# The end of a hybrid decoder layer, redone by tokens: TensorE turns x1 and then y, one operation per part scales and adds, and one store changes its place in SyncE's order

## The reference, cut to what matters

```python
def rmsnorm(x, g):
    y = xf * lax.rsqrt(jnp.mean(xf * xf, axis=-1, keepdims=True) + EPS)
    return (y * g.astype(jnp.float32)).astype(x.dtype)

def ffn_sublayer(x, w_up, w_down, g_pre, g_post):
    h = rmsnorm(x, g_pre)
    a = jnp.square(jax.nn.relu(jnp.einsum('ntd,df->ntf', h, w_up)))
    return x + rmsnorm(jnp.einsum('ntf,fd->ntd', a, w_down), g_post)
```

## Time and profile before

| what | us |
|---|---|
| median of 3 runs | 2083.25 |
| lowest, highest | 2081.37, 2084.26 |
| profiled execution, its own time | 2083.59 |
| its span | 2081.9 |
| PE busy / DVE / ACT / POOL | 1975.1 / 1329.2 / 1223.2 / 945.8 |
| mean granted TensorE clock (share of full speed) | 0.964 |

### The profile page before, as it was taken

How to read it: one execution, slowest core, us unless ns; L and a number is a source line. 1 busy time by engine, 2 the same in 40 slices (tenths; PEclk the granted TensorE clock), 3 DMA queues, 4 the chain that set the end, 5 groups by cost and what they waited for, 6 DMA issues and landing times.

```text
span 2081.9 us, 39222 instructions
## 1 busy us (share of the span) xinstructions
PE 1975.1 (95%) x15342; PEld 1944.4 (93%) x15342; DVE 1329.2 (64%) x1958; ACT 1223.2 (59%) x1790; POOL 945.8 (45%) x646
## 2 busy tenths in 40 slices
PE   7999999899964999999999999989999999999995
PEld 7999999899944999999999999989999999999994
DVE  3455643522258777777777777666666666666676
ACT  5234421422224677777777777667777777777782
POOL 0000022211161767676767677544445555444574
PEclk9999998999966999999999999989999999999996
DMA  5421121242220565656566665875655555556532
GB/s 174 158 62 61 52 82 56 102 146 92 92 86 17 170 208 175 209 182 196 186 192 191 192 199 183 292 250 188 205 181 200 191 184 204 183 183 205 187 105 86
DMA packets 270767, 328.16 MB, mean 158 GB/s; under 512 B 8128, under 2 KB 236872, under 8 KB 268975
## 3 DMA queue, kind: packets, MB, share of 16 engines
q1 hardware_dynamic: 267104, 315.66, 46.6%
q10 hardware_dynamic: 3479, 9.99, 1.3%
HBM read 253.79 MB, written 74.22 MB: 158 GB/s over the span
## 4 chain that ended last, share of the span: by engine, by line
PE 91%; DVE 5%; POOL 1%; DMA 1%; issue 1%; ACT 0%; SPq 0%; DVEq 0%; POOLq 0%; ACTq 0%
PE banks L1968 21%; PE banks L1613 21%; PE banks L1970 21%; PE banks L1969 21%; PE banks L1758 1%; POOL sq_sum L699 1%; DVE xF L1556 1%; PE banks L1579 1%; PE banks L1728 1%; DMA mlp_kept<-mlp_sums 1%; PE banks L1746 1%; DVE x1T L1481 1%; DVE h_part L1497 1%; DVE h_sum L1492 0%; PE banks L1587 0%
## 5 line engine op out<-in xcount | busy, mean ns | idle before, releaser
L1968 PE MATMUL banks<-h_part,splits 128*128 128x272 f32 x1792 | 522.9, 292 | 28.4 <-DVE h_part L1497 17.1
L1968 PE MATMUL banks<-mlp_parts,splits 128*128 128x272 f32 x1792 | 518.4, 289 | 12.2 <-DVE y_sum L1450 11.4
L1970 PE MATMUL banks<-h_part,splits 128*128 128x272 f32 x1792 | 521.3, 291 | 0.0
L1969 PE MATMUL banks<-h_part,splits 128*128 128x272 f32 x1792 | 518.8, 289 | 0.0
L1970 PE MATMUL banks<-mlp_parts,splits 128*128 128x272 f32 x1792 | 518.1, 289 | 0.0
L1969 PE MATMUL banks<-mlp_parts,splits 128*128 128x272 f32 x1792 | 517.2, 289 | 0.0
L1968 PEld LDWEIGHTS banks<-h_part,splits 128*128 128x128 f32 x1792 | 340.3, 190 | 29.4 <-issue 20.2
L1968 PEld LDWEIGHTS banks<-mlp_parts,splits 128*128 128x128 f32 x1792 | 337.9, 189 | 12.5 <-issue 11.6
L1969 PEld LDWEIGHTS banks<-mlp_parts,splits 128*128 128x128 f32 x1792 | 342.1, 191 | 0.0
L1969 PEld LDWEIGHTS banks<-h_part,splits 128*128 128x128 f32 x1792 | 340.8, 190 | 0.0
L1970 PEld LDWEIGHTS banks<-h_part,splits 128*128 128x128 f32 x1792 | 340.0, 190 | 0.0
(11 more groups left out here) (234 smaller groups left out, 3469.7 us busy)
## 6 DMA issues: line engine op xcount, KB each, us to landing
raw_up<-in_w_up SPq DMA_DIRECT2D x128, 512.0 KB, 7.7
raw_down<-in_w_down SPq DMA_DIRECT2D x128, 512.0 KB, 4.4
mlp_parts<-mlp_kept SPq DMA_DIRECT2D x56, 1088.0 KB, 8.4
mlp_kept<-mlp_hi SPq DMA_DIRECT2D x32, 952.0 KB, 4.5
mlp_kept<-mlp_sums SPq DMA_DIRECT2D x32, 952.0 KB, 5.7
w_raw<-in_w_in SPq DMA_DIRECT2D x40, 512.0 KB, 3.6
w_raw<-in_w_out SPq DMA_DIRECT2D x32, 512.0 KB, 3.4
x_kept<-x1T SPq DMA_DIRECT2D x4, 1088.0 KB, 4.0
```

The source lines that it names most:

```text
L1968: nc.tensor.matmul(out, wh, xh, start=first, stop=False, skip_group_check=not STARTS[i])
L1969: nc.tensor.matmul(out, wh, xl, start=False, stop=False, skip_group_check=not STARTS[i])
L1970: ins = nc.tensor.matmul(out, wl, xh, start=False, stop=j == pairs - 1, skip_group_check=not STARTS[i])
```

## The change

1. `store_lo` of group 30 moves: it was behind all load parts of the first chunk, now it stands ahead of part 4.
2. In the last chunk DVE multiplies finished y tiles by g_last in place (`scale_y`, 14 operations in the loop, two behind the last product of each group's index 5, and 2 after the last product).
3. After the last product PE turns x1 (80 transposes) into token rows, with the sums over partitions put behind part 6, then turns y (80 more). Banks 0 to 6 are a ring, bank 7 holds the sums.
4. ACT copies 14 of the x1 parts to x1_tok, DVE 6. The scale per token stays a column per token block (rstd); it is not spread by PE any more.
5. Of the y parts DVE takes 13 with one operation each (bank * rstd + x1_tok); for the other 7 ACT copies with the scale and POOL adds. The 20 stores read x1_tok and wait for no buffer.

```diff
@@ load parts of the first chunk, SyncE
                 if i == 2:
                     store_hi(UP_GROUPS - 2)
+                if i == 4:
+                    store_lo(UP_GROUPS - 2)
                 sp.wait_ge(product_done, N_UP - NP + i // 2 + 1)
                 load_part(0, i)
-            store_lo(UP_GROUPS - 2)
@@ who reads which part
-        OWN_NORMED = (0, 3, 7, 11, 14)
+        Y_RING = 7
+        Y_PARTS = TOK * KT // 4
+        X1_DVE = (1, 3, 5, 11, 14, 17)
+        Y_POOL = tuple(range(0, Y_PARTS, 3))
+        X1_ACT = tuple(o for o in range(Y_PARTS) if o not in X1_DVE)
+        Y_DVE = tuple(o for o in range(Y_PARTS) if o not in Y_POOL)
@@ stores, SyncE
+            for o in range(Y_PARTS):
+                kg, c = divmod(o, TOK)
+                who, count = y_reader(o)
+                sp.wait_ge(y_added[who], count)
...
+                sp.dma_start(dst[:, kg * 512:(kg + 1) * 512], x1_part(o)).then_inc(y_stored, 16)
@@ GpSimd
-            gp.wait_ge(scale_ready, 4)
-            for kt in range(KT):
-                if kt not in OWN_NORMED:
-                    normalise_tile(y_sum[:, kt, :], norm_f)
+            for i, o in enumerate(Y_POOL):
+                who, count = x1_reader(o)
+                gp.wait_ge(x1_copied[who], count)
+                gp.wait_ge(y_scaled, i + 1)
+                nc.gpsimd.tensor_tensor(x1_part(o), x1_part(o), y_tmp[0:tok_rows[o % TOK], i, :], ALU.add).then_inc(y_added[0], 1)
@@ ScalarE
+            for i, o in enumerate(X1_ACT):
+                act.wait_ge(y_turned, o + 1)
+                nc.scalar.activation(x1_part(o), y_bank(o, o), ACT.Copy).then_inc(x1_copied[0], 1)
+                if i == 5:
+                    take_root(3)
+            act.wait_ge(rstd_ready, 4)
+            for i, o in enumerate(Y_POOL):
+                act.wait_ge(y_turned, Y_PARTS + o + 1)
+                c = o % TOK
+                nc.scalar.activation(y_tmp[0:tok_rows[c], i, :], y_bank(Y_PARTS + o, o), ACT.Copy,
+                                     scale=rstd[0:tok_rows[c], c:c + 1]).then_inc(y_scaled, 1)
@@ VectorE
+            def scale_y(m):
+                dve.wait_ge(sq_ready, 2 * KT + m + 1)
+                nc.vector.tensor_scalar(y_sum[:, m, :], y_sum[:, m, :], g_last[:, m:m + 1], None, ALU.mult).then_inc(y_ready, 1)
...
+                G, i = divmod(N, NP)
+                n = G - (ALL_G - OUT_PAIRS)
+                if i == 5 and n > 0:
+                    scale_y(2 * n - 2)
+                    scale_y(2 * n - 1)
...
+            copy_x1(X1_DVE[0])
+            scale_y(KT - 2)
+            scale_y(KT - 1)
+            copy_x1(X1_DVE[1])
+            copy_x1(X1_DVE[2])
+            sums_by_token(3, banks[:, Y_RING, :])
+            row_roots(3)
+            dve.wait_ge(rstd_ready, 4)
+            for o in X1_DVE[3:]:
+                copy_x1(o)
+            for o in Y_DVE:
+                dve.wait_ge(y_turned, Y_PARTS + o + 1)
...
+                nc.vector.scalar_tensor_tensor(out=x1_part(o), in0=y_bank(Y_PARTS + o, o), scalar=rstd[0:tok_rows[c], c:c + 1],
+                                               in1=x1_part(o), op0=ALU.mult, op1=ALU.add).then_inc(y_added[1], 1)
@@ TensorE
-            turn_sums(3, total=sqf_sum, tmp=sqf_tmp)
-            spread_scales(3)
+            for o in range(Y_PARTS):
+                if o >= Y_RING:
+                    who, count = x1_reader(o - Y_RING)
+                    pe.wait_ge(x1_copied[who], count)
+                if o == Y_RING:
+                    turn_sums(3, banks[:, Y_RING, :], sqf_sum, sqf_tmp)
+                turn_part(o, xF)
+            pe.wait_ge(y_ready, KT)
+            for o in range(Y_PARTS):
...
+                turn_part(Y_PARTS + o, y_sum)
```

More of the change, by code:

```diff
@@ L215, in hybrid_decoder @@
         sqf_sum = at("sqf_sum", F_AT + 2 * T * 4, [P, T])
[L216 to L218 removed]
+        y_tmp = at("y_tmp", F_AT + 3 * T * 4, [P, 7, 512])
+        x1_tok = at("x1_tok", H_AT + NP * DOWN_J * 2 * H * 4, [P, TOK, D])
+        assert F_AT + 3 * T * 4 + 7 * 2048 <= H_AT + NP * DOWN_J * 2 * H * 4
         banks = ctx.enter_context(nc.psum_tensor("banks", [P, 8, 512], F32))
@@ L341, in hybrid_decoder @@
         y_turned = sem("y_turned")
-        y_copied = [sem("y_copied_act"), sem("y_copied_dve")]
-        y_stored = [sem(f"y_stored{i}") for i in range(8)]
+        x1_copied = [sem("x1_copied_act"), sem("x1_copied_dve")]
+        y_scaled = sem("y_scaled")
+        y_added = [sem("y_added_pool"), sem("y_added_dve")]
+        y_stored = sem("y_stored")
         kept = sem("kept")
@@ L369, in hybrid_decoder, with x1_reader, y_reader, y_bank @@
         START_SPLITS = {0: 0, 5: 1, 7: 2, 11: 3}
-        OWN_NORMED = (0, 3, 7, 11, 14)
[L375 to L379, removed]
+        Y_RING = 7
[4 more added lines that the diff above has]
+        Y_DVE = tuple(o for o in range(Y_PARTS) if o not in Y_POOL)
+        def x1_reader(o):
+            return (1, X1_DVE.index(o) + 1) if o in X1_DVE else (0, X1_ACT.index(o) + 1)
+        def y_reader(o):
+            return (0, Y_POOL.index(o) + 1) if o in Y_POOL else (1, Y_DVE.index(o) + 1)
+        def y_bank(s, o):
+            return banks[0:tok_rows[o % TOK], s % Y_RING, :]
+        def x1_part(o):
+            kg, c = divmod(o, TOK)
+            return x1_tok[0:tok_rows[c], c, kg * 512:(kg + 1) * 512]
         pool_order = [3, 2, 1, 0]
@@ L588, in _ @@
                     sp.dma_start(xF[:, 4 * n:4 * n + 4, :], x1_kept[:, 4 * n:4 * n + 4, :]).then_inc(x1_moved[n], 16)
[L591 to L601, removed]
+            for o in range(Y_PARTS):
+                kg, c = divmod(o, TOK)
+                who, count = y_reader(o)
+                sp.wait_ge(y_added[who], count)
+                dst = (y_prompt[0, c * P:(c + 1) * P, :] if c < TOK - 1 else y_sample.rearrange("b t d -> (b t) d"))
+                sp.dma_start(dst[:, kg * 512:(kg + 1) * 512], x1_part(o)).then_inc(y_stored, 16)
+            sp.wait_ge(y_stored, 16 * Y_PARTS)
             sp.wait_ge(kept, 16 * 3)
@@ L1542, in _ @@
                     mlp_low(UP_GROUPS - 1)
[L1545 to L1569, removed]
@@ L1978, in _, with turn_part @@
             pe.wait_ge(taken, N_ALL)
-            turn_sums(3, total=sqf_sum, tmp=sqf_tmp)
-            spread_scales(3)
-            pe.wait_ge(scale_ready, 4)
-            for kg in range(KT // 4):
-                for a in range(4):
-                    pe.wait_ge(y_ready, 4 * kg + a + 1)
-                    for c in range(TOK):
-                        o = kg * TOK + c
-                        r = tok_rows[c]
-                        if o >= 8 and a == 0:
-                            who, count = copier(o - 8)
-                            pe.wait_ge(y_copied[who], count)
-                        ins = nc.tensor.transpose(banks[0:r, o % 8, a * P:(a + 1) * P], xF[:, 4 * kg + a, c * P:c * P + r], ident[:])
-                        if a == 3:
-                            ins.then_inc(y_turned, 1)
+            for one in x1_moved:
+                pe.wait_ge(one, 32)
+            def turn_part(s, source):
+                kg, c = divmod(s % Y_PARTS, TOK)
+                r = tok_rows[c]
+                for a in range(4):
+                    ins = nc.tensor.transpose(y_bank(s, s % Y_PARTS)[:, a * P:(a + 1) * P],
+                                              source[:, 4 * kg + a, c * P:c * P + r], ident[:])
+                ins.then_inc(y_turned, 1)
+            for o in range(Y_PARTS):
[7 more added lines that the diff above has]
+            for o in range(Y_PARTS):
+                if o < Y_RING:
+                    who, count = x1_reader(Y_PARTS + o - Y_RING)
+                    pe.wait_ge(x1_copied[who], count)
+                else:
+                    who, count = y_reader(o - Y_RING)
+                    pe.wait_ge((y_scaled, y_added[1])[who], count)
+                turn_part(Y_PARTS + o, y_sum)
 _INS = ['x_prompt', 'x_sample', 'cache_k', 'cache_v', 'state_pool', 'w_in', 'w_out', 'w_pool', 'pool_scale', 'attn_sinks',
```

17 lines of the change are left out of this document (6 added, 11 removed).

## The result

The changed kernel takes 2060.72 us (median of 4 runs, 2059.18 to 2061.8), the kernel before in the same measurement 2083.48. The ratio is 0.9892, 95% interval 0.9875 to 0.9909: 22.8 us, 1.1%, faster. 2061.5 was forecast. The profiled execution took 2061.8 with a span of 2060.1 (before 2081.9) at a mean granted clock of 0.974 (before 0.964).

The account below looks back on a forecast made before the run. TensorE was taken as the bound through both weight stages, with no engine full in the end. Terms -8.8, +2.0 and -14.9 sum to -21.7; forecast 2061.5 us at 60%, own range 2055.5 to 2066, 8-in-10 range 2055.5 to 2070.5.

Parts of the forecast that it names:

- The moved store: Change from up to down: store lands at 1349.6 instead of 1358.4, DVE's squaring and all behind it earlier; -8.8 us.
- nothing was to be counted for the loads behind: Down stage start: three loads behind the store land some 2.5 us later, at most 0.7 us late; counted as nothing.
- The multiplications: Last chunk: a POOL operation between two DVE multiplications makes TensorE wait 0.35 us, six times; +2.0 us.
- the 2.65 us operation: Earlier profile: 272-column DVE operation, all operands in SBUF, begun while POOL worked; said to end with POOL's operation.
- The end: Behind the last product: new chain to the span's end, set by the stores, 29.7 us instead of 45.6; -14.9 us.
- the 1.0 set aside for the clock: Behind the last product: allowance of 1.0 us in case the clock falls behind the sums' one-column matmuls.
- The 0.65 us for a combination: Behind the last product: each of DVE's 13 combinations for y parts takes 0.65 us.
- Half clock to the end: Behind the last product: TensorE stays at half clock, the end gains only 2.4 us; 2074.1 us, 13%.
- The store landing before DVE asks: Change from up to down: queue shorter than counted, store gains 12.0 us; 2058.3 us, 13%.
- the store gaining nothing: Change from up to down: store not served before the loads behind it; 2070.3 us, 6%.
- DVE's combinations meeting POOL's additions: Behind the last product: 13 combinations at 1.77 us each, the end at 38.1 us; 2069.0 us, 6%.
- DVE falling behind in the last chunk: Last chunk: each multiplication waits out a POOL operation, TensorE loses 3.4 us per group and clock; 2091.6 us, 2%.

Follow-up runs that it names:

- the experiment: Changed kernel with each pair of the last chunk's multiplications made one group later, the last pair left in place; 2059.6 us, ratio 0.9889 to the kernel before.

## Why the forecast held

The time was right to 0.8 us, in part by luck: errors of up to 1.4 us, of both signs, cancelled, one of them (+1.05 in front of the change) being chance.

**The moved store, -8.8 against -7.7.** The mechanism was right: issue with the end of mlp_low, landing in the queue's turn, squaring at once, TensorE 2.0 later (1.97). What was mis-sized is the landing, 9.5 us behind the issue instead of 8.5. The store itself landed 2.7 us behind part 3, nearly the 2.5 that were counted; the rest is that part 3's landing was taken over unchanged from the earlier trace rows. It came 11.6 us behind its issue instead of 10.8, which looks as if the store's packets had begun beside part 3's; no run shows that. And the rate was lower with a store among the loads:

```profile
1342.20:1345.00 2.80, 2.80 (x25) 2.80 (x24) 2.38 (x5) 2.05 (x5) 1.14 (x1) 1.00 1.05 396
1345.00:1348.00 3.00, 3.00 (x26) 3.00 (x26) 1.31 (x3) 1.31 (x3) 1.30 (x1) 1.00 0.97 328
1348.00:1351.70 3.70, 2.15 (x18) 1.93 (x16) 0.00 (x0) 1.75 (x3) 0.00 (x0) 1.00 1.08 386
```

328 GB/s for three microseconds, where 399 had been counted: half a microsecond. That nothing was to be counted for the loads behind held: TensorE's second wait (1.68) is one on DVE, as forecast, and with the store put back behind all loads it is 1.69, so the three loads behind the store have no part in it.

**The multiplications, +2.0 against +0.6.** The mechanism was right again, POOL's operation between the two halves of a pair, and one of them only. The term was mis-sized in two places: the pair took 1.96 where 2.30 had been laid out, since POOL's operation began 0.2 after DVE's first and not behind it (of the 2.65 us operation the prediction says that it ended with POOL's; by the earlier trace rows it ended 0.3 behind it, as the multiplication here); and a take and a low part in a row move DVE on by 0.95 (2010.26 to 2011.21) and not by the 1.12 of their durations, as one is begun before the other is written down as ended. Together 0.5 us, more than the 0.35 of wait that each of six groups was to pay. That a multiplication is 0.43 us was nearly right (0.49 to 0.51 alone).

**The end, -14.9 against -15.7.** The chain came out as laid down: 0.58 before the first transpose, 3.1 for the first seven parts, 2.0 for the sums, 5.7 for the other x1 parts, the first store issued 14.2 behind the last take (13.9 forecast), the stores gapless at 322 to 347 GB/s, 1.8 behind the last data. Only the 1.0 set aside for the clock was not needed: with 28 transposes in front, sums of 2.0 us left it at 1.00. The 0.65 us for a combination, for which the prediction names no row, held (13 in 8.64 us). No run takes the new end further apart: what the missing spreading of the scale and the combinations from PSUM are worth each for itself is worked out from rows and not tested. The lower end of the stated range adds up to 2055.2 and not 2055.5, which changes nothing.

**The rivals.** Half clock to the end: no, 1.00 throughout. The store landing before DVE asks, and the store gaining nothing: no, DVE waited 4.22 us where near 3 was forecast. DVE's combinations meeting POOL's additions: no, 732 ns each with POOL at work beside them,

```profile
L794 POOL TENSOR_TENSOR x_tok<-x_tok,y_tmp 128x512 f32<-128x512 f32 (+1 forms) x7 | 8.9, 1273 | 10.5 <-ACT y_tmp L1087 10.3
L1585 DVE SCALAR_TENSOR_TENSOR x_tok<-banks,rstd,x_tok 128x512 f32<-128x512 f32 (+1 forms) x13 | 8.6, 732 | 1.1 <-PE banks L2002 1.1
```

where four combinations had taken 7.08 in the kernel before. That the operand in PSUM makes the difference fits this and the earlier trace rows; no run changes the operand alone. DVE falling behind in the last chunk: no. What came nearest to it is the 2.03 us pair of the experiment, and that cost 0.7 in one group.

## What to carry to other kernels

A store that frees a buffer somebody is about to write belongs in the queue behind only as many loads as the reader needs before that moment; count the queue's content at its issue, and look at what the loads behind it will then hold up. Where an end is bound by stores, its length is the time to the first store plus the transfer, so make the first output early rather than all of it fast; and put work that needs no one in front of a matmul that must wait, since an idle TensorE can cost the clock as well as the wait. What a fallen clock costs depends on what comes next: some 1.6 us where nothing waited behind it (686.5 against 684.9 in the two traces of the store ahead of part 3), nothing where TensorE had to wait for DVE soon after. When a DVE operation with all operands in SBUF has to stand beside POOL, place it in POOL's gap, and check the last round, where POOL does something else.

## What the runs showed of the hardware that was not expected

- After TensorE had been idle for 2.8 us the clock stayed at 1.00 for another microsecond of work and only then fell to 0.50, for some 7 us. In the wait of 3.65 us at the change from up to down it fell while TensorE was still idle (0.95 on average from 1352.0 to 1353.8, 0.50 from there to 1357). A wait of 1.89 us left it at 1.00 in one execution (matmuls of 0.36 and 0.29 us behind it), while in another it fell with a wait of 1.94 us (0.57), after waits of 0.50 and 1.12.
- With one store of 952 KB among the loads the queue's rate fell some 2 us behind the store's issue, in each kernel that had it there: 328 GB/s over 3 us in the changed kernel, 297 over 2 us with the store alone moved, 290 to 297 over 4 us with the store one load further ahead, against 391 in that stretch of the kernel before. Why was not tried.
- A kernel's part in front of an edit isn't the same in two executions: the same code reached the moved store's issue anywhere from 1338.5 to 1344.3 us. Stretches of a trace leave that part out, but one trace isn't enough either: for the same edit, the store ahead of part 3, they gave 3.1 us in one measurement and 1.2 in the other.
